# Seven products in place of eight in 16 of the 44 block pairs of the two down projections

## Chip, cores and metric

The kernel runs on one core of one Trainium2 chip. The metric is the device time of one execution in microseconds (us). Of the kernel before there are three runs (median 2378.72 us, 2378.43 to 2379.81) and one profiled execution.

## What is computed

Two transformer blocks on 256 tokens of width 2048, all in float32. The first one mixes (a Mamba-2 head group and a pooling mixer), then comes the gated feed-forward layer that this change touches, then a gated per-layer embedding; the second block is one layer of gated attention and one of retention. Cut to what matters:

```python
def conv_glu(hn, w_up, conv_w, conv_b, w_down):      # hn (256, 2048), w_up (2048, 2*5632), w_down (5632, 2048)
    gate, val = jnp.split(hn @ w_up, 2, axis=-1)
    gate = dwconv_centred(gate, conv_w, conv_b)
    return (jax.nn.gelu(gate, approximate=True) * val) @ w_down
...
h = h + rmsnorm(mix, mix_norm_post)
ff = conv_glu(rmsnorm(h, ffn_norm_pre), w_ffn_up, ffn_conv_w, ffn_conv_b, w_ffn_down)
h = h + rmsnorm(ff, ffn_norm_post)
gate = jax.nn.sigmoid(rmsnorm(h, ple_norm_pre) @ w_ple_gate)
h = h + rmsnorm(gate * (p @ w_ple), ple_norm_post)
```

## The kernel before

**Three products for one.** Every float32 product is made of three TensorE matmuls: each operand is split into a high part (rounded to the fp32r format) and a low part (the rest), and the kernel adds high x high, low x high and high x low in PSUM. Activations (`xa`, `xb`, `xc`) hold both parts side by side; `ff` tile k, 128 of the 5632 inner channels, lies in `xb` or `xc`.

**Pieces.** All weights stream from HBM in one order, `layout()`: the list `uses`, 813 pieces of 128 x 1024 numbers. For piece i SP loads it into `raw[i % 4]` (L624) once the low part of piece i-4 is made; ScalarE makes the high part `whi[i % 6]` (L1049, L1054) once TensorE is done with piece i-6; VectorE makes the low part `wlo[i % 6]` = raw - whi (L1520, L1505: a helper, so most tensor_tensor rows carry that line); TensorE's matmuls of pieces have L702. Each engine runs its own program, a loop over the pieces u: it first makes the split of piece u + 5, then the steps that `at[u]` lists for this point (`late(u, ...)` puts them there). So the order on every engine is fixed by hand, and a step that waits holds up what is behind it on its engine, splits too.

**The feed-forward layer** comes in two halves of 22 `ff` tiles. The up projection of a half has 11 gate and 11 val blocks of four pieces. GpSimd scales them and multiplies gate and value (`gate_scale`, `val_scale`, `val_gate`), VectorE does the convolution taps and the low parts (`val_low`), ScalarE the gelu and the high parts (`val_high`). The last val block of a half is finished by steps placed 1 to 4 pieces into the down projection.

**The down projection** of a half (`down0`, `down1`; `natural_out`, L125) has four blocks c of 512 output columns; a piece holds two k-tiles of one block, and gives 2 k x 2 token halves x 3 = 12 matmuls of 512 columns. Each block has two tiles, token halves t = 0 and 1, in two of the banks 0 to 3 (`bank[n % 4]`, n counts tiles); the first matmul of tile n waits until tile n-4 is evacuated (`emptied`). Banks 4 to 7 are idle there. ScalarE copies `down0` tiles to `sn` (L1275), VectorE adds the `down1` tiles to it (L1939), ScalarE squares the sum, VectorE multiplies it by the norm's row (`weigh`, L1607; the row is loaded into `X` and `ev` by `load_post`, L665).

**Behind it** four `ple` blocks of one piece each run (their tiles need the `down1` banks). VectorE meanwhile finishes the norm and makes the new h (`grow`, L1620, destination hT), TensorE transposes its 128x512 quads (`rms_turn`, L779, L793), the first two after the second ple piece, and the gate projection `pgate` starts on them.

## Time and profile before

| | us |
|---|---|
| median of 3 runs | 2378.72 |
| profiled execution, its own time | 2378.37 |
| its span, first to last instruction | 2376.6 |
| TensorE busy | 2361.9 (11890 matmuls) |
| VectorE busy | 1522.0 |
| ScalarE busy | 1195.6 |
| GpSimd busy | 266.2 |

Times in the rows are us from the start of the span. A row of the timeline gives the start, the length, the engine and line, the operation, output and inputs with their shapes, a count where equal neighbours are merged, and in brackets the idle time before it with who ended it. Neighbouring instructions of an engine overlap by some 0.1 us, so spacing says more than duration. PE is TensorE, DVE VectorE, ACT ScalarE, POOL GpSimd.

### The profile page before, as it was taken

How to read it: one execution, taken by the hardware profiler on the slowest of the kernel's cores; microseconds unless marked ns; L12 is line 12 of the kernel's file. 1: busy time of each engine (PE TensorE's matmuls, PEld its weight loads, DVE VectorE, ACT ScalarE, POOL GpSimd, SP SyncE). 2: the span in 40 equal slices, each digit the busy share in tenths (PEclk: the TensorE clock that was granted, in tenths of full speed). 3: DMA queues.
4: the chain of work that ended last, by engine and by line, in shares of the span. 5: the costliest groups of instructions: out<-in, count | busy, mean ns of one | idle time of the engine just before them, and what ended most of it. 6: DMA issues, size and time to landing. Idle time of an engine off the chain costs nothing.

```text
span 2376.6 us, 29824 instructions
## 1 busy us (share of the span) xinstructions
PE 2361.9 (99%) x11890; PEld 1982.9 (83%) x11890; DVE 1522.0 (64%) x1965; ACT 1195.6 (50%) x1613; POOL 266.2 (11%) x250
## 2 busy tenths in 40 slices
PE   9999999999999999999999999999999999999999
PEld 7878898888888888888788888887888888888887
DVE  7898577675467775575755556657665554656556
ACT  7876454444444444465655555535444444444442
POOL 1262013321013221000000000001000000000000
PEclk9999999999999999999999999999999999999999
DMA  8446656656665666565566565565665666556653
GB/s 297 156 145 198 215 176 195 188 191 192 193 193 187 188 193 207 191 203 175 176 185 205 158 196 162 167 190 164 191 181 180 214 192 197 177 182 182 189 177 125
DMA packets 122940, 444.04 MB, mean 187 GB/s; under 512 B 13744, under 2 KB 15408, under 8 KB 122288
## 3 DMA queue, kind: packets, MB, share of 16 engines
q1 hardware_dynamic: 122800, 442.12, 59.6%
q8 instruction: 94, 1.54, 0.3%
q14 instruction: 46, 0.38, 0.0%
HBM read 439.97 MB, written 2.10 MB: 186 GB/s over the span
## 4 chain that ended last, share of the span: by engine, by line
PE 93%; DVE 4%; ACT 2%; DMA 1%; issue 1%; SPq 0%; DVEq 0%; ACTq 0%
PE bank L702 92%; DVE wlo L1505 1%; DMA raw<-in_w 1%; DVE ev L1508 1%; ACT whi L1054 1%; PE bank L793 0%; DVE hT L1508 0%; DVE hn L1508 0%; PE bank L978 0%; PE bank L1045 0%; DVE xa L1508 0%; ACT hT L1222 0%; PE bank L1000 0%; DMA hT<-in_xT 0%; ACT L1228 0%
## 5 line engine op out<-in xcount | busy, mean ns | idle before, releaser
L1505 DVE TENSOR_TENSOR wlo<-raw,whi 128x1024 fp32r<-128x1024 f32 (+2 forms) x811 | 1012.9, 1252 | 771.2 <-ACT whi L1054 769.2
L1054 ACT ACTIVATE whi<-raw 128x1024 fp32r<-128x1024 f32 (+1 forms) x813 | 854.7, 1054 | 958.9 <-PE bank L702 942.4
L702 PE MATMUL bank<-xa,whi 128*128 128x512 f32 (+1 forms) x2688 | 841.5, 395 | 6.9 <-DVE xa L1508 3.5
L702 PE MATMUL bank<-whi,xa 128*128 128x512 f32 x2048 | 639.4, 393 | 2.2 <-DVE wlo L1505 1.8
L702 PEld LDWEIGHTS bank<-xa,wlo 128*128 128x128 f32 x2656 | 497.5, 188 | 115.0
L702 PE MATMUL bank<-xa,wlo 128*128 128x256 f32 (+1 forms) x2656 | 520.9, 278 | 0.0
L702 PE MATMUL bank<-whi,xb 128*128 128x512 f32 x1536 | 473.8, 390 | 0.0
L702 PEld LDWEIGHTS bank<-whi,xa 128*128 128x128 f32 x2048 | 379.7, 188 | 82.6 <-issue 4.7
L702 PEld LDWEIGHTS bank<-xa,whi 128*128 128x128 f32 x2688 | 411.0, 188 | 16.1 <-issue 6.6
L702 PE MATMUL bank<-wlo,xa 128*128 128x512 f32 x1024 | 399.1, 390 | 0.0
L702 PEld LDWEIGHTS bank<-whi,xb 128*128 128x128 f32 x1536 | 287.3, 188 | 59.3 <-DVE wlo L1505 0.3
L702 PE MATMUL bank<-wlo,xb 128*128 128x512 f32 x768 | 298.9, 389 | 0.0
L702 PEld LDWEIGHTS bank<-wlo,xa 128*128 128x128 f32 x1024 | 192.2, 188 | 41.1
L702 PEld LDWEIGHTS bank<-wlo,xb 128*128 128x128 f32 x768 | 144.1, 188 | 30.3
L2176 POOL TENSOR_TENSOR S<-S,rs 128x256 f32<-128x256 f32 x88 | 103.4, 1198 | 552.7 <-DVE S L1518 439.3
L2176 POOL TENSOR_TENSOR ev<-ev,con 128x256 f32<-128x256 f32 x32 | 40.6, 1288 | 563.4 <-DVE ev L1518 563.4
L2176 POOL TENSOR_TENSOR hn<-hn,hT 128x512 f32<-128x512 f32 x4 | 7.8, 1972 | 725.0 <-DVE xa L1505 724.9
L702 PE MATMUL bank<-whi,xc 128*128 128x512 f32 x224 | 69.1, 390 | 0.0
L1518 DVE TENSOR_REDUCE S<-bank 128x256 f32<-128x512 f32 x88 | 56.4, 681 | 0.9 <-PE bank L702 0.6
L702 PEld LDWEIGHTS bank<-whi,xc 128*128 128x128 f32 x224 | 41.9, 188 | 8.6
L1518 DVE TENSOR_REDUCE ev<-bank 128x256 f32<-128x512 f32 (+1 forms) x66 | 42.5, 683 | 5.7 <-PE bank L702 5.7
L702 PE MATMUL bank<-wlo,xc 128*128 128x512 f32 x112 | 43.6, 389 | 0.0
(244 smaller groups left out, 1264.5 us busy)
## 6 DMA issues: line engine op xcount, KB each, us to landing
raw<-in_w SPq DMA_DIRECT2D x803, 512.0 KB, 3.8
hT<-in_ln_rows SPq DMA_DIRECT2D x2, 2048.0 KB, 8.3
raw<-in_w SPq DMA_DIRECT2D x9, 256.0 KB, 2.8
X<-in_post SPq DMA_DIRECT2D x3, 768.0 KB, 5.5
S<-in_x SPq DMA_DIRECT2D x4, 512.0 KB, 7.8
hT<-in_x SPq DMA_DIRECT2D x1, 2048.0 KB, 8.2
out<-S SPq DMA_DIRECT2D x8, 256.0 KB, 2.5
hT<-in_xT SPq DMA_DIRECT2D x3, 512.0 KB, 6.8
```

Of the source, the lines that this page charges most:

```text
L702: return pe.matmul(o, w, x, start=start, stop=stop, skip_group_check=True)
L1054: act.activation(hi, r, ACT.Copy).then_inc(*w_high(i))
L1505: return dve.tensor_tensor(o, x, y, op)
L1508: return dve.scalar_tensor_tensor(out=o, in0=x, scalar=s, in1=y, op0=op0, op1=op1)
L1518: return dve.tensor_reduce(o, halves(b), AX, ALU.add)
L2176: return pool.tensor_tensor(o, x, y, op)
```

## The change

In both halves `natural_out` gives way to `paired_out`. It takes two neighbouring blocks c together. For four of the eleven k-pairs (`COMBINED`) the 2 x 2 x 2 products (two token halves, two k-tiles, two blocks of columns) are replaced by seven products of sums (the Strassen-Winograd scheme). With the k-tiles' weights as `upper` and `lower`, each with two halves of 512 columns, a group is: `upper` (1 product), `lower` (2), a plain piece, `pair_sums` (2), `full_sums` (2), a plain piece; the remaining k-pairs are plain pieces (2 or 3 ahead of the groups, two in each group, 4 or 3 behind). GpSimd makes the weight sums from the raw pieces (`sums`, four 128x512), ScalarE and VectorE split them as if they were pieces. The `upper` piece is split in its first 512 columns alone. GpSimd also makes the sums of activations (`mixed`, one 128x512 and four 128x128 for each k-pair and half); those of k-pairs 0 and 1 in the up projection, of 2 and 3 in the down projection. Four of the seven products collect in banks 4 to 7; behind the last group `fold` and `fold_end` combine them. In the first half VectorE writes them to `sn` and then adds the tiles there itself (ScalarE does not copy `down0` tiles any more); in the second half they go to a part of `xa`'s space (`wide`) and GpSimd adds them to `sn` (`joined`). The sums of the second half and the norm's row 1 lie in `xa`'s space too. The list has 845 pieces, 813 of them loaded.

```diff
+Use = namedtuple("Use", "mat col k0 n cols block first last part", defaults=("",))
+SUMS = ("pair_sums", "full_sums")
+COMBINED = (0, 1, 2, 3)
+EARLY = (0, 1)
+IN_PAIRS = (0, 1)
...
+    def paired_out(kind, operand, mat, k, start, groups, end):
+
+        begun = len(uses) - 1
+        for c in (0, 2):
+            pair = [begin(kind, c + j, operand, "natural", 512) for j in range(2)]
+            touched, left = set(), [(j, p) for j, p in start + sum([g[1:] for g in groups], ()) + end]
+
+            def plain(j, p):
+                b = pair[j]
+                left.remove((j, p))
+                first, last = j not in touched, j == 1 and (1, p) == end[-1]
+                touched.add(j)
+                use(b, mat, 512 * (c + j), k + 2 * p, 2, first, last)
+
+            def part(name, row, col, first, last=False):
+                uses.append(Use(mat, 512 * (c + col), row, 1, 1024, pair[0], first, last, name))
+                return len(uses) - 1
+
+            for piece in start:
+                plain(*piece)
+            for p, one, two in groups:
+                first, last, row = p == groups[0][0], p == groups[-1][0], k + 2 * p
+                a = part("upper", row, 0, first)
+                late(max(a - 7, begun + 2) if k else a - 7, "sums", a)
+                part("lower", row + 1, 0, first)
+                plain(*one)
+                part("pair_sums", row, 0, first)
+                d = part("full_sums", row, 0, first, last)
+                plain(*two)
+            late(d + 1, "fold", kind, c, d)
+            late(d + 2, "fold_end", kind, c)
+            late(d + 2, kind, pair[0])
+            for piece in end:
+                plain(*piece)
+            assert not left
+        return len(uses) - 1
+
+    def mix(u, half, p):
+        late(u, "mixed", half, p)
+        late(u + 2, "mixed_high", half, p)
...
+            if half in IN_PAIRS and q in EARLY:
+                mix(e + d + 5, half, q)
...
+        if half in IN_PAIRS:
+            n = 2 + half
+            for i, p in enumerate(COMBINED):
+                if p not in EARLY:
+                    mix(len(uses) + n + 6 * (i - 1) - 5, half, p)
+            turns = tuple((j, p) for j in range(2) for p in range(4, 11))
+            ends["down", half] = paired_out(f"down{half}", ("ff",), "w_ffn_down", 22 * half, turns[:n],
+                                            tuple((p, turns[n + 2 * i], turns[n + 2 * i + 1]) for i, p in enumerate(COMBINED)),
+                                            turns[n + 8:])
...
-    late(d - 40, "load_post", 1)
+    late(d - 50, "load_post", 1)
...
+        sums = {0: (X[:, 0:1024], flat(ev[:, 0:4, :])), 1: (wide[:, 0:1024], wide[:, 1024:2048])}
+        mixed_x, mixed_v = flat(sq[:, :, :]), s2[:, 3584:4096]
...
+        def folded(kind, c, t, j):
+            if kind == "down1":
+                return wide[:, 2048 + 1024 * t + 512 * j:2560 + 1024 * t + 512 * j]
+            return sn[:, t, 512 * (c + j):512 * (c + j) + 512]
...
+            w = 512 if s.part == "upper" else s.n * s.cols
+            r = (sum_piece(i) if s.part in SUMS else raw[turn_of[i] % NRAW])[:, 0:w]
+            hi, lo_ = whi[i % NHL][:, 0:w], wlo[i % NHL][:, 0:w]
...
+                    if uses[before].part == "upper":
+                        q.wait_ge(*pool_val.of("sum", before, 2))
+                    elif uses[before].part == "lower":
+                        q.wait_ge(*pool_val.of("sum", before - 1, 4))
+                sp.dma_start(raw[turn % NRAW][:, 0:n], src).then_inc(raw_in[turn % NRAW], 16)
...
+                        if r == 1:
+                            q.wait_ge(*piece_tile.of("used", XA_FREE[1]))
+                            for i in range(2):
+                                sp.dma_start(wide[:, 4096 + 1024 * i:5120 + 1024 * i],
+                                             a["post"][1:2, 1024 * i:1024 * i + 1024].broadcast_to((128, 1024))).then_inc(post_in, 16)
+                            continue
...
+                def product(B, x, c, start, stop=False):
+                    xh, xl = x
+                    mm(B[:, :], xh, hi[:, 512 * c:512 * c + 512], start)
+                    mm(B[:, :], xl, hi[:, 512 * c:512 * c + 512], False)
+                    return mm(B[:, :], xh, lo_[:, 512 * c:512 * c + 512], False, stop)
...
+                if s.part == "upper":
+                    m = product(bank[5], tokens(s.k0, 0), 0, side_free(5), s.last)
+                elif s.part == "lower":
+                    product(bank[n % 4], tokens(s.k0, 0), 0, begins(0))
+                    m = product(bank[(n + 2) % 4], mixture(4), 1, begins(2))
+                elif s.part == "pair_sums":
+                    product(bank[6], mixture(1), 0, side_free(6), s.last)
+                    m = product(bank[4], mixture(3), 1, side_free(4), s.last)
+                else:
+                    product(bank[7], mixture(2), 0, side_free(7), s.last)
+                    m = product(bank[(n + 1) % 4], tokens(s.k0 + 1, 1), 1, begins(1), s.last)
+                m.then_inc(*piece_tile.both(*([("tile", n), ("tile", n + 1)] if s.last else []), ("used", u)))
...
+                if uses[i].part == "pair_sums":
+                    q.wait_ge(*pool_val.of("sum", group_of(i), 2))
+                elif uses[i].part == "full_sums":
+                    q.wait_ge(*pool_val.of("sum", group_of(i), 4))
+                else:
+                    q.wait_ge(*landed(i))
                 if i >= NHL:
                     q.wait_ge(*piece_tile.of("used", i - NHL))
                 act.activation(hi, r, ACT.Copy).then_inc(*w_high(i))
...
+                    elif step == "mixed_high":
+                        half, p = k
+                        q.wait_ge(*pool_val.of("mixed", half, p, 4))
+                        act.activation(mixed_set(half, p)[:, 0, :], mixed_v, ACT.Copy).then_inc(*x_high("mixed", 11 * half + p))
+                    elif step == "fold":
+                        kind, c, d = k
...
+                        q.wait_ge(*piece_tile.of("used", d))
+                        act.activation(folded(kind, c, 0, 0), bank[5][:, :], ACT.Copy).then_inc(*act_evac("first", kind, c))
...
+                    elif step == "mixed_low":
+                        half, p = k
+                        m = mixed_set(half, p)
+                        q.wait_ge(*x_high.of("mixed", 11 * half + p))
+                        tt(m[:, 1, :], mixed_v, f32(m[:, 0, :]), ALU.subtract).then_inc(*x_low("mixed", 11 * half + p))
+                    elif step == "fold":
+                        kind, c, d = k
+                        x = [[folded(kind, c, t, j) for j in range(2)] for t in range(2)]
+                        q.wait_ge(*act_evac.of("first", kind, c))
+                        tt(x[0][1], bank[7][:, :], x[0][0], ALU.subtract).then_inc(*vec_val("less", kind, c))
+                        q.wait_ge(*vec_val.now())
+                        tt(x[1][0], x[0][1], bank[4][:, :], ALU.add).then_inc(*vec_val("fold", kind, c, 0))
+                    elif step == "fold_end":
+                        kind, c = k
+                        x = [[folded(kind, c, t, j) for j in range(2)] for t in range(2)]
+                        q.wait_ge(*vec_val.of("fold", kind, c, 0))
+                        tt(x[0][1], x[0][1], bank[6][:, :], ALU.add).then_inc(*vec_val("fold", kind, c, 1))
+                        tt(x[1][1], x[1][0], bank[6][:, :], ALU.add).then_inc(*vec_val("folded", kind, c))
+                    elif step == "down0" and 0 in IN_PAIRS:
+                        c = k[0].arg
+                        q.wait_ge(*vec_val.of("folded", "down0", c - c % 2))
+                        for t in range(2):
+                            n = k[0].tile + t
+                            x = sn[:, t, 512 * c:512 * c + 512]
+                            q.wait_ge(*piece_tile.of("tile", n))
+                            if t and c % 2 == 0:
+                                tt(x, bank[n % 4][:, :], x, ALU.subtract).then_inc(*vec_evac("tile", n))
+                            else:
+                                tt(x, x, bank[n % 4][:, :], ALU.add).then_inc(*vec_evac("tile", n))
...
+                            if 1 in IN_PAIRS:
+                                q.wait_ge(*pool_val.of("joined", "down1", c - c % 2))
...
+                    elif step == "mixed":
+                        half, p = k
...
+                        tt(r, f32(x[:, :, 0:T]), f32(x[:, :, T:2 * T]), ALU.add).then_inc(*pool_val("mixed", half, p, 0))
+                        upper, lower = mixed_x[:, 0:T], mixed_x[:, T:2 * T]
+                        v = [mixed_v[:, 128 * i:128 * i + 128] for i in range(4)]
+                        q.wait_ge(*pool_val.now())
+                        tt(v[0], upper[:, 128:256], lower[:, 128:256], ALU.subtract).then_inc(*pool_val("mixed", half, p, 1))
+                        tt(v[2], upper[:, 128:256], upper[:, 0:128], ALU.subtract).then_inc(*pool_val("mixed", half, p, 3))
+                        q.wait_ge(*pool_val.of("mixed", half, p, 1))
+                        tt(v[1], upper[:, 0:128], v[0], ALU.subtract).then_inc(*pool_val("mixed", half, p, 2))
+                        q.wait_ge(*pool_val.now())
+                        tt(v[3], lower[:, 0:128], v[1], ALU.subtract).then_inc(*pool_val("mixed", half, p, 4))
+                    elif step == "sums":
...
+                        if earlier:
+                            q.wait_ge(*w_low.of(earlier[-1]))
+                        if uses[a].first and uses[a].col == 0:
+                            q.wait_ge(*(x_low.of("p", 1) if uses[a].block.kind == "down0" else piece_tile.of("used", XA_FREE[1])))
+                        up, low = [raw[turn_of[i] % NRAW] for i in (a, a + 1)]
+                        q.wait_ge(*landed(a))
+                        tt(pair[:, 0:512], up[:, 0:512], up[:, 512:1024], ALU.add).then_inc(*pool_val("sum", a, 1))
+                        q.wait_ge(*landed(a + 1))
+                        tt(pair[:, 512:1024], up[:, 512:1024], low[:, 512:1024], ALU.add).then_inc(*pool_val("sum", a, 2))
+                        q.wait_ge(*pool_val.of("sum", a, 1))
+                        tt(full[:, 0:512], pair[:, 0:512], low[:, 512:1024], ALU.add).then_inc(*pool_val("sum", a, 3))
+                        q.wait_ge(*pool_val.now())
+                        tt(full[:, 512:1024], full[:, 0:512], low[:, 0:512], ALU.add).then_inc(*pool_val("sum", a, 4))
+                    elif step == "fold_end" and k[0] == "down1":
...
+                                q.wait_ge(*vec_val.of("folded", kind, c))
+                                m = tt(x, x, folded(kind, c, t, j), ALU.subtract if (t, j) == (1, 0) else ALU.add)
+                        m.then_inc(*pool_val("joined", kind, c))
```

## Rows read from the trace of the kernel before

**Rows 1.** Page, busy time of TensorE and others, and the granted clock by slice.
```profile
PE 2361.9 (99%) x11890; PEld 1982.9 (83%) x11890; DVE 1522.0 (64%) x1965; ACT 1195.6 (50%) x1613; POOL 266.2 (11%) x250
...
PEclk9999999999999999999999999999999999999999
```
**Rows 2.** Page, the chain that ended last, by engine.
```profile
PE 93%; DVE 4%; ACT 2%; DMA 1%; issue 1%; SPq 0%; DVEq 0%; ACTq 0%
```
**Rows 3.** Timeline of TensorE, two products of the second down projection.
```profile
1031.79 0.61 PE L702 MATMUL bank<-whi,xc 128*128 128x512 f32 x2
1032.24 0.39 PE L702 MATMUL bank<-wlo,xc 128*128 128x512 f32 x1
1032.47 0.61 PE L702 MATMUL bank<-whi,xc 128*128 128x512 f32 x2
1032.92 0.39 PE L702 MATMUL bank<-wlo,xc 128*128 128x512 f32 x1
```
**Rows 4.** Timeline of VectorE, two low parts of the second down projection.
```profile
942.02 1.23 DVE L1505 TENSOR_TENSOR wlo<-raw,whi 128x1024 fp32r<-128x1024 f32 x1 [1.49 <-ACT whi L1054]
944.74 1.23 DVE L1505 TENSOR_TENSOR wlo<-raw,whi 128x1024 fp32r<-128x1024 f32 x1 [1.49 <-ACT whi L1054]
```
**Rows 5.** Timeline of ScalarE, splits behind the second up projection.
```profile
916.45 1.06 ACT L1054 ACTIVATE whi<-raw 128x1024 fp32r<-128x1024 f32 x1 [1.67 <-PE bank L702]
919.17 1.06 ACT L1054 ACTIVATE whi<-raw 128x1024 fp32r<-128x1024 f32 x1 [1.66 <-PE bank L702]
```
**Rows 6.** Windows: length, then PE, PEld, DVE, ACT, POOL busy; second up and down projection.
```profile
661.00:914.00 253.00, 253.00 (x1444) 220.42 (x1443) 174.53 (x220) 112.35 (x136) 64.64 (x62) 1.00 0.61 189
914.00:1033.00 119.00, 119.00 (x527) 98.54 (x526) 63.19 (x61) 51.90 (x59) 4.85 (x4) 1.00 0.64 202
```
**Rows 7.** Timelines of VectorE and GpSimd, and the tile view of hn (min/median/max ns).
```profile
1644.34 10.10 DVE L1505 TENSOR_TENSOR wlo<-raw,whi 128x1024 fp32r<-128x1024 f32 x5 [0.26 <-ACT whi L1054]
1644.22 8.01 POOL L2176 TENSOR_TENSOR hn<-hn,hT 128x512 f32<-128x512 f32 x4 [724.86 <-DVE xa L1505]
L2176 POOL TENSOR_TENSOR hn<-hn,hT x4: 1304/2154/2276, 1644.2 to 1650.1; 128x512 f32<-128x512 f32 x4
```
**Rows 8.** Timelines of VectorE and GpSimd, end of the second up projection (913.7).
```profile
912.61 1.22 DVE L1505 TENSOR_TENSOR wlo<-raw,whi 128x1024 fp32r<-128x1024 f32 x1
913.74 1.28 DVE L1518 TENSOR_REDUCE S<-bank 128x256 f32<-128x512 f32 x2
914.94 1.38 DVE L1505 TENSOR_TENSOR wlo<-raw,whi 128x1024 fp32r<-128x1024 f32 x1
914.51 2.42 POOL L2176 TENSOR_TENSOR S<-S,rs 128x256 f32<-128x256 f32 x2 [8.65 <-DVE S L1518]
916.88 2.48 POOL L2176 TENSOR_TENSOR S<-S 128x256 f32<-128x256 f32 x2
329.74 0.74 POOL L2176 TENSOR_TENSOR S<-S,rs 128x256 f32<-128x256 f32 x1
```
**Rows 9.** Page, DMA issues: count, size, median us to landing.
```profile
raw<-in_w SPq DMA_DIRECT2D x803, 512.0 KB, 3.8
```
**Rows 10.** Groups of VectorE in the second down projection: count, busy, mean ns.
```profile
L1505 DVE TENSOR_TENSOR S<-S,bank 128x512 f32<-128x512 f32 x7 | 4.5, 678 | 0.0
```
**Rows 11.** Timelines of VectorE, ScalarE, TensorE, end of the second down projection.
```profile
1032.92 1.28 DVE L1505 TENSOR_TENSOR S<-S,bank 128x512 f32<-128x512 f32 x2
1034.39 1.31 DVE L1505 TENSOR_TENSOR S<-S,ev 128x512 f32<-128x512 f32 x2 [0.19 <-ACT sq L1101]
1036.39 2.06 DVE L1508 SCALAR_TENSOR_TENSOR hT<-S,sm,hT 128x512 f32<-128x512 f32 x3
1031.76 1.28 ACT L1285 ACT_TABLE_LOAD   x1
1038.59 0.60 PE L793 MATMUL bank<-con,hT 128*128 128x128 f32 x4
```

139 lines of the change are left out of this document (120 added, 19 removed).

## Prediction, made before the changed kernel ran

> **What bounds the kernel now.** I read the page first: TensorE is busy for 2361.9 of 2376.6 us and the clock row shows the upper level (2.4 GHz) in every slice [rows 1]; the chain that ended last is 93% TensorE [rows 2]. So a matmul taken out is worth its spacing, if nothing else gets late. In the timeline of a down projection three matmuls of 512 columns start every 0.68 us, 0.227 us each, 2.72 us for a piece of twelve [rows 3]. VectorE makes one low part per piece and then sits idle 1.49 us for ScalarE, which waits for TensorE to give back a buffer [rows 4, 5]. The splits thus stand at the end of their lead: a piece is split six pieces ahead. The lead, not the mean idle share, is what the change has to live on: it is 16.3 us of TensorE before the change, less the two splits.
>
> Then I looked for GpSimd and VectorE together, because the change gives GpSimd its first work in the down projections (it is idle in the window of the second, after the last two gates) [rows 6]. One place in the trace has wide two-input work on both: GpSimd does four 128x512 operations while VectorE does four low parts and then one more. Alone, a low part occupies 1.13 us (its 1.22 us less the overlap with the next). In this place five of them take 10.10 us, four of them 8.96 us together, 2.24 us each; GpSimd's take a median of 2.15 us and the first 1.30 us [rows 7]. So 1.13 + 1.11 = 2.24: they don't overlap at all, they alternate, one whole instruction each. The end of the second up projection repeats it with 256 columns: the low part at 914.94 takes 1.38 us instead of 1.22 us, and two GpSimd operations 2.42 us, though that form takes 0.74 us where nothing delays it [rows 8]. Reductions that read a bank (913.74) are not stretched.
>
> **What is removed.** Sixteen groups (4 k-pairs, 2 column pairs, 2 halves) need 7 x 3 = 21 matmuls in place of 24: 48 x 0.227 = 10.9 us off TensorE. A group with its two plain pieces has 45 matmuls, 10.2 us. The pieces brought from HBM do not grow in number, and one piece lands in 3.8 us [rows 9].
>
> **What is added to each group.** VectorE: before, four low parts in 10.9 us; now upper (half width, 0.6 us) and lower, one, pair, full, two at 1.13: 6.25 us. GpSimd: four sums of 128x512 at 1.11 us, 4.4 us. Side by side both fit in 10.2 us. As they alternate they need 10.7 us, and there is a loop: the sums of a group wait for the low part of the full sums of the group before (one pair of buffers), and that comes last in VectorE's order. Call the end of that low part F. Without other work F to F is 10.7 to 11.4 us against 10.2; over three steps this costs 1.5 to 3.5 us of a lead of some 9 us. In the second column pair of each half I therefore take nothing (up to 2 us).
>
> **The mixtures left in the down projection** (k-pairs 2 and 3, in the first column pair). Each is a 128x512 and four 128x128 on GpSimd. No row shows a 128x128 there; from 1.11 us for 512 columns and 0.60 us for 256 (the second of the pair in rows 8 ran 0.6 us after the low part ended at 916.32) I get about 0.35 us as an estimate. With the low part of the mixture (0.6 us) the port is asked for 3.1 us more, 13.8 us in such a group. And ScalarE stands in order: the high part of the mixture is queued before the split of pair_sums, so that split, then its low part, start only when the mixture is done: 0.55 + 1.06 us [rows 5] with the port empty. Written out with alternating operations, F to F is 16.3 us (with the two low parts of the last values) and then 15.5 us, against 10.2.
> First half, time from the end of the up projection: the sums of group 1 were made in the up projection, F1 = 5.2 us (used(e+1) at 2.72, high, low), F2 = 21.5, F3 = 37.0. The plain piece of group 4 is then ready after 4 sums and 4.0 us of low parts, at 45.3 us. TensorE would want it at 5.4 + 3 x 10.2 + 2.0 = 38.1. **Loss 7.2 us.** Bounds: if the port never idled 1.8 us, if every sum met a low part 10 us.
> Second half: the sums lie in xa's place and cannot start before the up projection ends, and GpSimd still has the last values, until 4.6 us [rows 8]. Then two sums, split, two sums, split: F1 = 12.7 us, wanted at 14.3. F2 = 29.1, F3 = 44.6, the plain piece 52.9 us, wanted at 8.2 + 30.6 + 2.0 = 40.8. **Loss 12.1 us.** Bounds 6.6 and 16 us. This is the largest term; it shows as waits of TensorE on VectorE of 0.5 to 3 us before lower, one and pair_sums.
> The mixtures of k-pairs 0 and 1 are made in the up projection, where in 253 us VectorE is busy for 175 us [rows 6]; a GpSimd step there is needed four pieces later. Cost nothing; if that cover were gone, 3 us each.
>
> **A rule on this.** The Trainium skill (SBUF — State Buffer, "SBUF: two separate sides") says that a VectorE operation with two SBUF inputs and a GpSimd operation that reads SBUF take one pair of ports exclusively, for the whole instruction. By that rule the sum stands as here; the trace agrees (2.24 us for the pair). If ports were shared freely, the two losses above would be zero.
>
> **Folding, second half.** The output of the first half lies in sn, so GpSimd adds the folded banks to it (four 128x512, "joined"), and VectorE's evacuation of the first block waits for that; low parts are queued behind it on VectorE, squares and splits behind it on ScalarE. From the end of the last combined piece: high and low of the next piece 2.2 us, fold copy, two operations of 0.68 us [rows 10] 3.6, next split 4.9, two more 6.3 us; GpSimd is then still at the sums of the next column pair, which are queued ahead and whose pieces land at 3 and 4.5 us, until 8 to 9.2 us; joined 4 x 1.1 to 1.2: 13 us; evacuation 13.7 us. TensorE has four plain pieces, 10.9 us, then wants that bank. **Loss 3.0 us** (2 to 5). In the first half nothing waits for GpSimd here: evacuated by 8.8 us, wanted at 13.6.
> **At the end** no sums stand in the way: joined by 11.5 us, bank free at 12.3, wanted at 10.9: 1.4 us. But VectorE now comes late to the fourth block: evacuation of the third, weights, two splits, then the fourth at 16.8 us instead of 10.7. From the first evacuation at 1032.92 to the end of the first grown quad (a third of the 2.06 us from 1036.39) are 4.2 us, and the transposes at 1038.59 had only 1.5 us to spare [rows 11]. They move from 16.3 to about 21.3 us. **Loss 5.0 us** with the 1.4 (3 to 8). What is late next is the table load of 1.28 us on ScalarE before the squares [rows 11], hidden behind the splits.
>
> Moves with one answer: the norm row goes to xa's place, the same bytes on SP's queue, ten pieces into the second down projection (some 22 us), wanted first by the weights behind the first folding (46 us): nothing. Evacuations of the first half go from ScalarE to VectorE, 8 x 0.68 us where it idles 1.49 us per piece: nothing.
>
> **Sum.** Against the profiled execution, 2378.4 us (span 2376.6, 1.8 around it; the median of the runs is 2378.7): 2378.4 - 10.9 + 7.2 + 12.1 + 3.0 + 5.0 = **2394.8 us**. Lower bounds 1.8 + 6.6 + 2 + 3 give 2380.9; upper ones 10 + 16 + 5 + 8 give 2406.
>
> **Rivals.** Differences within 0.2%, 4.8 us, count as no change.
> A, faster: the sums and low parts overlap after all, for instance because GpSimd reads other buffers than VectorE. It speaks for it that rows 7 and 8 are few; against it, that they also have different buffers on the two engines (hn and raw, S and raw). Then F to F is 4.4 + 1.06 + 1.13 = 6.6 us, the groups lose nothing, and only the foldings stay, some 1.5 + 3: 2372 us. If even these are hidden 2367.5 us. It decides once F to F is under the lead's allowance, about 12 us for a group with a mixture. Chance 0.10.
> B, the lead covers the groups (the port is fair but GpSimd's operations fall into VectorE's idle time), and the foldings cost their 8 us: 2375.5 us, or a few us more with a part of the second half's loss. For it: VectorE idles 55% of a plain piece. Against it: in a group VectorE's and GpSimd's work is 10.7 of 10.2 us. Chance 0.14.
> C, forecast: the shared port stretches the first column pair of both halves: 2381 to 2405 us, 2395 likeliest. Chance 0.70.
> D, worse: the sums come late in the second column pairs too, since loads wait for sums (raw slots of upper and lower are held until the second and fourth sum, then 3.8 us), so that each of eight more groups loses 1 to 2 us: 2405 to 2412 us. Chance 0.06.
> That fewer matmuls are removed than said: the page must count 11842 in place of 11890; the blocks of the diff give that number, so I leave it no chance of its own.
> The range reaches over B and C: 2375 to 2405. Faster 0.10 (A, most of it), within 0.2% 0.16 (B and the low edge of A and C), slower 0.74.
>
> **What will show it.** Low parts in the groups at 2.2 us beside sums of 2.2 us, and at 1.2 us elsewhere: the port. TensorE's waits on VectorE's low parts in the first 50 us of both down projections, more in the second (7 and 12 us), next to none in the second column pairs: the loop. One wait on an evacuation, 3 us, at the change of column pair in the second half, and one before the ple blocks; first transposes 5 us later relative to the last down matmul: the folding. No TensorE idle time in the first column pairs would make the forecast wrong; sums of 1.2 us beside low parts of 1.2 us would tell why.

## The result, and the profile after

| | before | after |
|---|---|---|
| median of 4 runs | 2379.26 us | 2407.09 us (2406.81 to 2408.38) |
| profiled execution | 2378.4 us, span 2376.6 | 2408.4 us, span 2406.6 |
| matmuls | 11890 | 11842 |

The changed kernel is slower: the ratio is 1.0117, 95% interval 1.0105 to 1.0130. The forecast was 2394.8 us with a range of 2375 to 2405, and the measured time lies above it, at a time that the prediction had given to its rival D. The sign held, the size did not: 16 us of loss were foreseen and 28 came. The page of the kernel after, its busy times and its clock:

```profile
PE 2364.6 (98%) x11842; PEld 1977.8 (82%) x11842; DVE 1626.4 (68%) x2029; ACT 1218.4 (51%) x1649; POOL 429.8 (18%) x362
...
PEclk9999999999999999999999999999999999999999
```

Against [rows 1] there are 48 matmuls fewer, so the change does what it says, and TensorE is nevertheless "busy" 2.7 us longer. The difference between span and busy time of TensorE went from 14.7 to 42.0 us. VectorE has 104 us more work and GpSimd 164 us.

**Where the time lies.** The two stages that the change touches, as windows (length, then busy time of PE, PEld, DVE, ACT, POOL, the granted clock of TensorE, DMA share, GB/s): the first down projection, and the second one with the ple blocks up to the first transposes.

```profile
550.05:673.40 123.35, 117.75 (x506) 95.33 (x505) 106.39 (x82) 61.24 (x68) 65.45 (x42) 0.99 0.55 181
918.60:1067.50 148.90, 128.07 (x531) 101.61 (x529) 111.56 (x96) 68.41 (x87) 79.35 (x54) 0.95 0.52 170
```

Before, the same two stages took 119.7 us (528 matmuls) and 125.1 us (the transposes at 1038.59 [rows 11]). 504 matmuls are worth 114.3 us, so the first one now holds 9.1 us in which TensorE waited or ran slowly; of the second, 119.7 us are matmuls and 29.2 us are loss. The second up projection between them takes 245.2 us in both traces. In each stage the loss is its length less its matmuls at 0.2267 us. The sum for the profiled execution: 2378.4 - 10.9 (matmuls) + 9.1 + 29.2 + 1.5 (a stretch at 181 us, below) + 1.0 (behind the transposes) = 2408.3 us, against 2408.4.

**The waits.** TensorE's timeline of after, only its rows that carry a wait (start, length, instruction, then the idle time ahead and what ended it). The first column pair of the first half, then that of the second half, the change of column pair of the second half, and its end:

```profile
571.46 0.73 PE L824 MATMUL bank<-whi,xs 128*128 128x512 f32 x2 [0.82 <-DVE wlo L1712]
580.50 0.74 PE L824 MATMUL bank<-whi,xc 128*128 128x512 f32 x2 [0.57 <-DVE wlo L1712]
587.66 1.22 PE L824 MATMUL bank<-whi,xs 128*128 128x512 f32 x2 [4.11 <-DVE wlo L1712]
...
938.81 0.73 PE L824 MATMUL bank<-whi,xb 128*128 128x512 f32 x2 [1.48 <-DVE wlo L1712]
941.04 0.73 PE L824 MATMUL bank<-whi,xb 128*128 128x512 f32 x2 [1.26 <-DVE wlo L1712]
946.59 0.73 PE L824 MATMUL bank<-whi,xs_ev 128*128 128x512 f32 x2 [1.15 <-DVE wlo L1712]
955.63 0.72 PE L824 MATMUL bank<-whi,xb 128*128 128x512 f32 x2 [0.57 <-DVE wlo L1712]
962.80 1.07 PE L824 MATMUL bank<-whi,xa 128*128 128x512 f32 x2 [4.14 <-DVE wlo L1712]
...
996.88 1.19 PE L824 MATMUL bank<-whi,xb 128*128 128x512 f32 x2 [8.37 <-DVE S L1712]
...
1058.83 1.19 PE L824 MATMUL bank<-whi,xc 128*128 128x512 f32 x2 [2.55 <-DVE S L1712]
1064.13 0.70 PE L824 MATMUL bank<-whi,xc 128*128 128x512 f32 x2 [0.85 <-DVE S L1712]
1067.57 0.65 PE L973 MATMUL bank<-con,hT 128*128 128x128 f32 x4 [0.45 <-DVE hT L1715]
```

"DVE wlo" is a low part that was late: the loop of sums and splits. "DVE S" is an evacuation into sn, so a bank that was not yet free: the folding. The bracket leaves out the end of the matmul before; measured from start to start less one spacing, the four large waits cost 4.3, 4.3, 8.5 and 2.7 us. The second column pairs have no wait inside them. Cut at these rows, with 252 matmuls (57.1 us) to a column pair and 24 to the two ple pieces, the 29.2 us of the second stage are 12.5 us in the first column pair, 10.6 us at the change (8.5 of wait and 2.1 behind it) and 6.0 us at the end, to 0.1 us.

**The port.** Timelines of VectorE and GpSimd of after inside a group of the second half:

```profile
948.19 7.39 DVE L1712 TENSOR_TENSOR wlo<-raw,whi 128x1024 fp32r<-128x1024 f32 x4
948.35 3.92 POOL L2418 TENSOR_TENSOR wide<-raw 128x512 f32<-128x512 f32 x2 [4.69 <-DVE wlo L1712]
952.24 4.49 POOL L2418 TENSOR_TENSOR wide<-wide,raw 128x512 f32<-128x512 f32 x2
```

The single low parts inside the first row, at 951.05 and 953.28, take 2.31 and 2.30 us, the sums at 952.24 and 954.58 take 2.27 and 2.15; elsewhere a low part takes 1.22 us as in [rows 4]. It is the picture of [rows 7].

**The change of column pair.** GpSimd of after from 973 to 996 us; then SP's queue and VectorE at the rows that decide when those sums can start; and one group of the view of waits between 950 and 1000 us (who waited for what: us in total, times, longest):

```profile
984.99 1.29 POOL L2418 TENSOR_TENSOR wide<-raw 128x512 f32<-128x512 f32 x1 [12.06 <-DMA raw<-in_w]
986.79 1.74 POOL L2418 TENSOR_TENSOR wide<-raw 128x512 f32<-128x512 f32 x1 [0.50 <-DMA raw<-in_w]
988.48 2.60 POOL L2418 TENSOR_TENSOR wide<-wide,raw 128x512 f32<-128x512 f32 x2
991.04 4.92 POOL L2418 TENSOR_TENSOR S<-S,wide 128x512 f32<-128x512 f32 x4
...
973.00 0.33 SPq L747 DMA_DIRECT2D raw<-in_w  x1
977.78 2.49 DVE L1712 TENSOR_TENSOR wlo<-raw,whi 128x1024 fp32r<-128x1024 f32 x2 [0.23 <-ACT whi L1239]
980.30 0.33 SPq L747 DMA_DIRECT2D raw<-in_w  x1
982.41 0.33 SPq L747 DMA_DIRECT2D raw<-in_w  x1
...
SPq L448 <- POOL wide L2418: 14.0, 5, 4.1
```

The last combined piece was used at about 977.5 us. The folded banks were complete 11 us behind that, at 988.6. GpSimd began the next column pair's sums 7.5 us behind it, because their first piece landed only then (the second at 9.3 us); its four additions to sn ended at 995.96, and VectorE evacuated at 996.05. Why the pieces were late can be followed through the slots. The last sum of the group before ended at 972.93, and only then was the slot of lower free: SP issued the next load at 973.00 and the one queued behind it right after. These two pieces landed, were split, and their low parts ended at 980.27 (the row at 977.78). The slot of the second was the one that the next column pair's upper needed, so its load went out at 980.30 and landed at 984.99; that of lower went out at 982.41, behind one more low part. So two loads stand one behind the other between the last sum of one column pair and the first of the next, and GpSimd has nothing to do for 12.06 us. The row of SP's queue has the held loads: five times one waited for a sum, up to 4.1 us.

**The clock.** Not foreseen: behind each of the four large waits TensorE runs at half its clock. Windows of after: before the wait, right behind it, and a little later; then behind the wait that ended at 587.66.

```profile
980.00:988.00 8.00, 8.00 (x37) 6.64 (x36) 6.22 (x8) 3.56 (x4) 2.51 (x2) 1.00 0.88 301
996.90:1000.50 3.60, 3.60 (x9) 2.83 (x10) 3.23 (x5) 2.67 (x6) 0.00 (x0) 0.50 0.10 8
1002.00:1010.00 8.00, 8.00 (x37) 6.58 (x36) 6.58 (x8) 6.01 (x10) 2.64 (x2) 1.00 0.49 149
587.70:591.00 3.30, 3.30 (x8) 2.62 (x9) 3.30 (x4) 2.96 (x4) 1.57 (x1) 0.51 0.00 0
```

A granted clock of 0.50 is the lower level, 1.2 GHz; a matmul of 512 columns then starts every 0.43 us instead of 0.227. Such a stretch costs 1.6 to 1.8 us here, together 6.7 of the 38.3 us. The view counts these matmuls as busy, which is why PE's busy time grew while its work shrank. The page's row of the clock, in slices of 60 us, doesn't show it. The 1.5 us ahead of the first down projection are the same thing: at 181.5 us, in code that the change doesn't touch, this execution ran at 0.50 for some 3 us behind a wait with 1.55 us of idle time, and the profiled execution of before did not. Other kernels below have it in some executions too; it is no effect of the change.

### The profile page after: what moved, and what is told of

It reads as the page before. It is cut to its first block, busy times and chain, and to the rows that moved or that the text cites. A ratio compares the mean times of both kernels' runs of the same rounds, so it can differ in the third digit from the quotient of the medians.

```text
span 2406.6 us, 30013 instructions
## 1 busy us (share of the span) xinstructions
PE 2364.6 (98%) x11842; PEld 1977.8 (82%) x11842; DVE 1626.4 (68%) x2029; ACT 1218.4 (51%) x1649; POOL 429.8 (18%) x362
## 4 chain that ended last, share of the span: by engine, by line
PE 54%; DVE 1%; ACT 0%; issue 0%; DVEq 0%; ACTq 0%
PE bank L824 53%; DVE wlo L1712 0%; DVE hn L1715 0%; PE bank L1225 0%; PE bank L1158 0%; PE bank L973 0%; PE bank L1180 0%; ACT whi L1239 0%; DVE xa L1712 0%; DVE S L1712 0%; ACT S L1268 0%; DVE sm L1760 0%; ACT wide L1287 0%; PE bank L1005 0%; ACT L1536 0%
## 5 line engine op out<-in xcount | busy, mean ns | idle before, releaser
L1712 DVE TENSOR_TENSOR wlo<-raw,whi 128x1024 fp32r<-128x1024 f32 (+2 forms) x811 | 1047.1, 1299 | 656.0 <-ACT whi L1239 654.0
L1239 ACT ACTIVATE whi<-raw 128x1024 fp32r<-128x1024 f32 (+2 forms) x813 | 844.1, 1045 | 864.0 <-PE bank L824 823.0
L824 PE MATMUL bank<-whi,xa 128*128 128x512 f32 x2080 | 650.6, 394 | 6.5 <-DVE wlo L1712 5.9
L824 PEld LDWEIGHTS bank<-whi,xa 128*128 128x128 f32 x2080 | 386.2, 188 | 89.4 <-DVE wlo L1712 7.0
L824 PE MATMUL bank<-whi,xb 128*128 128x512 f32 x1376 | 426.8, 391 | 11.7 <-DVE S L1712 8.4
L824 PE MATMUL bank<-wlo,xa 128*128 128x512 f32 x1040 | 406.0, 390 | 0.0
L824 PEld LDWEIGHTS bank<-whi,xb 128*128 128x128 f32 x1376 | 257.7, 188 | 68.0 <-issue 8.8
L824 PE MATMUL bank<-wlo,xb 128*128 128x512 f32 x688 | 268.6, 390 | 0.0
L824 PEld LDWEIGHTS bank<-wlo,xb 128*128 128x128 f32 x688 | 129.5, 188 | 27.2
```

The costliest lines, as they stand in the source:

```text
L824: return pe.matmul(o, w, x, start=start, stop=stop, skip_group_check=True)
L1239: act.activation(hi, r, ACT.Copy).then_inc(*w_high(i))
L1712: return dve.tensor_tensor(o, x, y, op)
```

## Experiments

The kernel before ran beside each of them, with a median between 2378.6 and 2379.3 us. Ratios are against it, with 95% intervals. "Cost" of a wait is start to start less one spacing, plus the slow stretch behind it.

Theory: in the first column pair of each half VectorE's and GpSimd's operations alternate on one port, and the late mixtures (k-pairs 2 and 3) push the loop over what TensorE's work covers; the foldings add their waits in the second half. Rival 1: the port is not the cause; buffers, loads or the order on ScalarE are. Rival 2: the change could not gain at all, since each microsecond saved comes back at a later wait.

### Each half by itself

```diff
-IN_PAIRS = (0, 1)
+IN_PAIRS = (0,)
```

> The changed kernel with the seven products in the first half alone; the second down projection is that of the kernel before. Theory (shared port of VectorE and GpSimd, and ScalarE's order, in the first column pair): the first half cost 9 us of waits for 5.4 us saved in the changed kernel's trace, so the kernel is 3 to 4 us slower than before: 2382 to 2384 us. Rival (the changed code outside the down projections costs too, such as the mixtures made in the up projection): 2385 us or more. Rival (the first half is a gain by itself): under 2377 us.

Measured 2388.6 us, 1.0041 (1.0026 to 1.0055): a miss. The first down projection was the same as in the changed kernel, and one more wait stood in the plain second one:

```profile
927.98 0.74 PE L824 MATMUL bank<-whi,xb 128*128 128x512 f32 x2 [3.78 <-DVE wlo L1712]
```

It is an artefact of the edit. The change lets the row's load stand 50 pieces before the end of the down projection; with the 44 whole pieces that the second one now has again, that place is six pieces inside the up projection. There SP waits for xa to be free, with all the later loads queued behind. The repeat puts only that back:

```diff
-    late(d - 50, "load_post", 1)
+    late(d - 40, "load_post", 1)
```

> Seven products in the first half alone, as before, but the norm row is loaded 40 pieces ahead of the end, not 50. In the kernel with 50 its wait for the end of the second up projection stood on SP's queue six pieces ahead of that end, as the second down projection is 44 pieces there. Theory: that is a mistake of that experiment, its wait of 4.2 us with the slow stretch behind it at the start of the second down projection goes, and what stays is the first half's own cost: 2382 to 2384 us. Rival (the change costs outside the down projections): 2386 us or more.

Measured 2382.1 us, 1.0014 (1.0005 to 1.0024). TensorE has three waits for low parts in the first down projection and none in the second. View of waits, first down projection of this kernel:

```profile
PE bank L824 <- DVE wlo L1712: 5.3, 3, 4.2
```

So the first half alone costs about 3 us (2.8 by the medians, 3.5 in the profiled execution, where the stage loses 8.9 us and 24 matmuls give back 5.4). The other 25 us belong to the second half. The pair also shows the price of a step moved past a queue: 6.5 us for the place of one load.

### The port alone

In the kernel before, GpSimd gets 32 operations of 128x512 in each down projection, four at a time, on a part of s2 that nobody else uses. Nothing waits for them within the stage.

```diff
+                    elif step == "extra":
+                        half, i = k
+                        q.wait_ge(*w_low.of(u))
+                        for n in range(4):
+                            q.wait_ge(*pool_val.now())
+                            tt(s2[:, 3584:4096], s2[:, 3584:4096], s2[:, 3584:4096], ALU.add).then_inc(*pool_val("extra", half, i, n))
```

> The kernel before, with 8 times four additions of 128x512 on GpSimd in each down projection, on a buffer that nothing else uses, once every five pieces (13.6 us). No engine waits for them. Theory: low parts beside them take 2.2 us in place of 1.2 us, and TensorE does not notice, since the lead of six pieces covers it and nothing is queued behind: 2378 to 2380 us. So the shared port alone, without the waits that the change builds on it, costs nothing. Rival (the port by itself delays TensorE): 2383 us or more.

Measured 2378.6 us, 0.9997 (0.9987 to 1.0006). VectorE and GpSimd of this kernel:

```profile
927.01 6.02 DVE L1508 TENSOR_TENSOR wlo<-raw,whi 128x1024 fp32r<-128x1024 f32 x3
936.57 1.82 DVE L1508 TENSOR_TENSOR wlo<-raw,whi 128x1024 fp32r<-128x1024 f32 x1 [1.50 <-ACT whi L1056]
925.76 6.18 POOL L2179 TENSOR_TENSOR S<-S 128x512 f32<-128x512 f32 x4
935.16 6.26 POOL L2179 TENSOR_TENSOR S<-S 128x512 f32<-128x512 f32 x4 [3.21 <-DVE wlo L1508]
```

GpSimd touches only its own buffer and VectorE's low parts are stretched all the same, three of them to 6.0 us instead of 3.5, and the operations of GpSimd to 1.5 us on average instead of 1.1. So they alternate on separate buffers too; rival A of the prediction had held it possible that they would not. By itself the stretching costs TensorE nothing: 1.22 us of low part per 2.72 us leave room. That it becomes a wait with a group's extra VectorE work and its loop is an inference: no run has the groups without the alternation. The Trainium skill's rule that was weighed in the prediction (SBUF — State Buffer, "SBUF: two separate sides": one engine has the pair for the whole instruction, the other is fully blocked) is borne out by these rows.

### The late mixtures

The mixtures of k-pairs 2 and 3 are left out, and their products read those of k-pairs 0 and 1; nothing else changes.

```diff
                 if p not in EARLY:
-                    mix(len(uses) + n + 6 * (i - 1) - 5, half, p)
+                    pass
...
-                    q.wait_ge(*x_low.of("mixed", s.k0 // 2))
-                    m = mixed_set(int(b.kind == "down1"), x)
+                    q.wait_ge(*x_low.of("mixed", 11 * int(b.kind == "down1") + x % 2))
+                    m = mixed_set(int(b.kind == "down1"), x % 2)
```

> The changed kernel without the mixtures of k-pairs 2 and 3 (20 GpSimd operations, 4 high and 4 low parts left out); their products read the mixtures of k-pairs 0 and 1 instead, so part of the down projections is computed from other numbers, with the same matmuls, weight sums and splits. Theory (mixtures on the shared port, and the split of pair_sums queued behind them on ScalarE, stretch the loop from 11 to 16 us): the waits of the first column pairs go almost whole (9 and 12 us), and as VectorE is no longer behind, the change of column pair in the second half costs 3 to 5 us in place of 10.7; the end costs its 6 us: 2379 to 2386 us. Rival (weight sums and raw slots held for them are the cause): it stays over 2395 us.

Measured 2389.4 us, 1.0043 (1.0028 to 1.0058), 17.7 us less than the changed kernel and outside the 2379 to 2386 expected. In the first down projection TensorE has no wait left: 114.3 us for its 504 matmuls. In the second the first column pair costs 2.7 us instead of 12.5. So four late mixtures cost TensorE 18.9 us in the first column pairs, and the sums without them 2.7 us. The edit takes out the mixtures' work on GpSimd, ScalarE and VectorE at once; it doesn't say which of the three weighs most. What I expected to shrink with them and did not is the wait at the change of column pair:

```profile
977.49 1.19 PE L824 MATMUL bank<-whi,xb 128*128 128x512 f32 x2 [8.69 <-DVE S L1712]
965.97 3.17 POOL L2418 TENSOR_TENSOR wide<-raw 128x512 f32<-128x512 f32 x2 [13.31 <-DMA raw<-in_w]
```

With its lead intact the wait is as long as before. GpSimd again starts the next sums 8.2 us after the last combined piece (at about 957.8), when their piece lands. So this wait does not come from lateness carried over; it is made on the spot.

Queueing only the high and low part of a late mixture three pieces later, so that ScalarE's split of pair_sums stands ahead of it:

```diff
+        d = 0 if p in EARLY else 3
-        late(u + 2, "mixed_high", half, p)
-        late(u + 3, "mixed_low", half, p)
+        late(u + 2 + d, "mixed_high", half, p)
+        late(u + 3 + d, "mixed_low", half, p)
```

> The changed kernel, but the high and low parts of the two late mixtures of each half are queued three pieces later on ScalarE and VectorE, behind the splits of pair_sums and full_sums. Theory (ScalarE's order holds up the split of pair_sums until the mixture is done): the loop of such a group shrinks by 2 to 3 us, four times: 8 to 12 us less in all, 2395 to 2399 us. Rival (only the port counts, and the same work stands on it): 0 to 4 us less, 2403 us or more.

Measured 2401.2 us, 1.0093 (1.0076 to 1.0110). The first down projection lost 7.2 us in place of 9.1, the first column pair of the second half 12.0 in place of 12.5, and the change of column pair 7.4 in place of 10.6; in all less than expected. The order on ScalarE is worth about a fifth of the first half's loss; in the second half, where the sums start later, hardly anything in the groups.

### The folding at the change of column pair

Three edits at this wait. First, the four additions to sn are made by VectorE right behind the folding, not by GpSimd behind the next sums:

```diff
                         tt(x[1][1], x[1][0], bank[6][:, :], ALU.add).then_inc(*vec_val("folded", kind, c))
+                        if kind == "down1":
+                            q.wait_ge(*vec_val.now())
+                            for t in range(2):
+                                for j in range(2):
+                                    y = sn[:, t, 512 * (c + j):512 * (c + j) + 512]
...
+                            m.then_inc(*vec_val("joined", kind, c))
```

> The changed kernel, but the four additions of the folded banks to sn in the second half are made by VectorE right behind the folding, not by GpSimd behind its weight sums. Theory (GpSimd's queue decides: 2.5 us of sums and 5 us of additions stand between folding and evacuation): the bank at the change of column pair is free 5 us earlier, at the end 2.7 us earlier, with the slow stretch of TensorE behind each wait shorter too: 9 to 11 us less, 2396 to 2398 us. Rival (VectorE's lateness decides, and 2.5 us more work on it makes that worse): 3 us less at most, 2404 us or more.

Measured 2402.8 us, 1.0101 (1.0086 to 1.0116): 4.3 us less than the changed kernel, not the 9 to 11 expected. At the change 6.00 us of idle time stayed, 9.1 us with the slow stretch, which was longer here (2.9 us). Second, GpSimd keeps the additions but makes them ahead of the next column pair's sums:

```diff
-                late(max(a - 7, begun + 2) if k else a - 7, "sums", a)
+                late((max(a - 7, begun + 2) if c == 0 else max(a - 7, d0 + 3)) if k else a - 7, "sums", a)
```

> The changed kernel, but in the second half GpSimd's additions of the folded banks at the change of column pair stand ahead of its weight sums for the next pair. In the changed kernel the sums waited for their pieces until 7.5 us after the last combined piece, ended at 13.6 us, and the additions at 18.5 us, while the folding was done at 11 us. Theory (two parts: pieces and so the folding late by loads held for sums, and GpSimd's queue): the queue's part is the 2.5 us between 11 and 13.6 us; the bank is free 2.5 us earlier and the rest of the wait, 6 us, stays: 2403 to 2406 us. Rival (the queue is all of it): the wait of 8.5 us and the slow stretch go, 2397 us or less.

Measured 2407.0 us, 1.0120 (1.0106 to 1.0134): nothing gained. TensorE of this kernel, the change of column pair and the end:

```profile
992.52 1.19 PE L825 MATMUL bank<-whi,xb 128*128 128x512 f32 x2 [5.49 <-DVE S L1713]
1057.34 1.19 PE L825 MATMUL bank<-whi,xc 128*128 128x512 f32 x2 [5.44 <-DVE S L1713]
```

Of 8.37 us of idle time at the change 5.49 stayed, about as expected, and the end went from 2.55 to 5.44 us: the 2.9 us won at the one place are lost at the other. (All times of this trace are 1.5 us earlier, for lack of the stretch at 181 us; with that taken off, the bank at the end came free at the same time as in the changed kernel, to 0.1 us.) What stays at the change are the additions themselves, behind a folding that is late, not GpSimd's queue; GpSimd of this kernel:

```profile
986.67 4.92 POOL L2419 TENSOR_TENSOR S<-S,wide 128x512 f32<-128x512 f32 x4 [15.28 <-DVE wide L1713]
```

They start with the end of the folding and end at 991.59, and TensorE's bank is free a microsecond later. Third, VectorE frees the bank first, adding it to the folded buffer, and adds to sn afterwards:

```diff
-                            q.wait_ge(*pool_val.of("joined", "down1", c - c % 2))
-                            tt(x, x, bank[n % 4][:, :], ALU.add).then_inc(*vec_evac("tile", n))
+                            x = folded("down1", c - c % 2, t, c % 2)
+                            tt(x, x, bank[n % 4][:, :], ALU.subtract if t and c % 2 == 0 else ALU.add).then_inc(*vec_evac("tile", n))
+                        for t in range(2):
...
+                            tt(x, x, folded("down1", c - c % 2, t, c % 2),
+                               ALU.subtract if t and c % 2 == 0 else ALU.add).then_inc(*vec_val("joined", c, t))
```

> The changed kernel, but in the second half VectorE adds the banks of a block to the folded buffer first (which frees them) and then adds the folded buffer to sn itself; GpSimd's additions are gone and no evacuation waits for another engine. Theory (the bank was held from the folding through GpSimd's weight sums and additions): the bank at the change of column pair is free at the folding, about when TensorE wants it, and at the end no bank is late: of the 10.3 and 6.5 us that these two places cost in the changed kernel's trace 1 to 2 us each stay: 2391 to 2394 us. Rival (VectorE, late because pieces land late, is what holds TensorE there whoever adds): 5 us less at most, 2402 us or more.

Measured 2400.9 us, 1.0090 (1.0075 to 1.0105): 6.2 us less than the changed kernel where 13 to 16 were expected. (The whole edit also moves the scratch of the squares out of xa's space and lets each square wait for the one before it.) TensorE in the first column pair of the second half, with the granted clock behind that wait; then at the change, soon behind it, and at the end:

```profile
940.49 1.22 PE L824 MATMUL bank<-whi,xb 128*128 128x512 f32 x2 [1.26 <-DVE wlo L1715]
...
940.50:943.20 2.70, 2.70 (x6) 2.14 (x7) 1.33 (x1) 0.06 (x1) 2.52 (x4) 0.50 0.76 259
...
988.99 0.70 PE L824 MATMUL bank<-whi,xb 128*128 128x512 f32 x2 [0.27 <-DVE wide L1715]
1001.94 1.22 PE L824 MATMUL bank<-whi,xb 128*128 128x512 f32 x2 [2.48 <-DVE wlo L1715]
1056.74 1.19 PE L824 MATMUL bank<-whi,xc 128*128 128x512 f32 x2 [3.23 <-DVE wide L1715]
```

Of the 10.6 us at the change half a microsecond stays, and 4.2 us come back at 1002 us (2.6 of wait and 1.6 at the lower clock): the low parts there are now late. Two causes are possible and not told apart: VectorE has four more additions queued ahead of them, and the wait at the change no longer gives the engines behind TensorE their lead back. About 2 us more are lost where the edit changes nothing, since the slow stretches behind the low parts' waits of the two first column pairs are longer or more in this execution (the row at 940.49 has one, the changed kernel at the same wait none).

### Fewer groups, where there is room

If the loop is the cause, fewer groups and a longer lead of whole pieces in the first column pair remove it. On top of the edit above: two groups (k-pairs 0 and 1, whose mixtures come from the up projection) behind six whole pieces in the first column pair, four groups in the second; the late mixtures are then made while whole pieces run. 36 matmuls fewer.

```diff
-                    mix(len(uses) + n + 6 * (i - 1) - 5, half, p)
+                    mix(len(uses) + 9 + 3 * (i - 2), half, p)
...
+            for ps, n in ((EARLY, 6), (COMBINED, n)):
+                turns = tuple((j, p) for j in range(2) for p in range(11) if p not in ps)
+                plans.append((turns[:n], tuple((p, turns[n + 2 * i], turns[n + 2 * i + 1]) for i, p in enumerate(ps)),
+                              turns[n + 2 * len(ps):]))
```

> As the kernel that frees the banks first, and with two groups (k-pairs 0 and 1) in the first column pair of each half, four in the second; mixtures 2 and 3 are made beside plain pieces. 12 groups, 36 matmuls fewer than before: 8.2 us. Theory (the waits came from mixtures between sums on the shared port, and from banks held): nearly no waits are left, 0 to 3 us: 2370 to 2374 us, faster than the kernel before. Rival (groups stretch TensorE by themselves, by loads held for sums): 2378 us or more.

Measured 2380.6 us, 1.0006 (0.9997 to 1.0015): 26.5 us less than the changed kernel, but above the 2370 to 2374 us expected, and not to be told from the kernel before. The first down projection is clean; the second has waits of 1.4 us inside and loses 6.5 us at its end, where the bank is late; that end was not in the expectation:

```profile
1035.90 1.19 PE L826 MATMUL bank<-whi,xc 128*128 128x512 f32 x2 [3.75 <-DVE wide L1717]
```

Fewer whole pieces at the start of the second column pair, so two or three more behind its groups to cover the last folding:

```diff
-            for ps, n in ((EARLY, 6), (COMBINED, n)):
+            for ps, n in ((EARLY, 6), (COMBINED, 2 - half)):
```

> The kernel with two and four groups and banks freed first, but its second column pairs begin with two plain pieces in the first half and one in the second, so that one or two pieces more stand behind the last group, 16.3 us of TensorE behind the folding in the second half in place of 10.9 us. Its trace had 6 us of waits left at the end of the second half, where VectorE came to the last bank 4 us late because folding, additions, squares and weights of the block before stood ahead. Theory (that queue): they go but for about 1 us, 2373 to 2376 us, faster than before by 3 to 6 us. Rival (the work of the end on VectorE is simply too much for the ple pieces to cover): 2379 us or more.

Measured 2381.4 us, 1.0011 (1.0002 to 1.0020). Again a miss. The end shrank from 6.5 to 3.2 us (1.2 before the bank, 2.0 before the transposes), and the groups, which have now a shorter lead, wait 4.2 us between 962 and 1008 in place of 1.4. In the second half 18 matmuls (4.1 us) bring 7.3 us of waits.

So the last two runs drop the second half altogether and keep two and four groups in the first one, where no sum waits for xa's place and no addition to sn is needed:

```diff
-IN_PAIRS = (0, 1)
+IN_PAIRS = (0,)
...
-    late(d - 50, "load_post", 1)
+    late(d - 40, "load_post", 1)
```

> The groups in the down projection of the first half only: two groups in its first column pair, behind six whole pieces, four in its second; the second down projection as before the change and the load of the row at d-40. 18 matmuls fewer (4.1 us). In the kernel with this order in both halves the first down projection ran without any wait, and everything that was lost stood in the second. So: 2378.8 - 4.1 = 2374.7, range 2373.5 to 2376.5. Rival (what is saved here comes back at a later wait whatever is done, as every kernel so far has ended at or above the time of the kernel before): 2377.5 to 2380.

Measured 2375.27 us, 0.9984 (0.9975 to 0.9993): 3.4 us faster than the kernel before, the only version that beats it, though by less than the 0.2% that the prediction calls a change. Its first down projection as a window, and below it the same stage in the kernel before:

```profile
550.30:666.30 116.00, 116.00 (x513) 95.79 (x512) 96.90 (x79) 58.80 (x64) 57.14 (x37) 1.00 0.60 195
...
548.50:668.20 119.70, 119.70 (x530) 99.14 (x529) 56.27 (x49) 50.95 (x53) 4.87 (x4) 1.00 0.63 192
```

TensorE is busy for all of it at full clock. VectorE is busy for 97 of 116 us, in the kernel before for 56 of 120. Rival 2 falls with this run: what is saved stays saved where nothing waits. The same with one more group in the first column pair, whose mixture must be made while groups run:

```diff
-            for ps, n in ((EARLY, 6), (COMBINED, n)):
+            for ps, n in (((0, 1, 2), 6), (COMBINED, n)):
```

> As the one with two and four groups in the first down projection alone, but three groups in its first column pair, behind the same six whole pieces: 21 matmuls fewer (4.8 us), and one mixture (k-pair 2) is formed and split while that column pair runs. By theory the port is then shared for one group of sums and one mixture longer, and the lead of six pieces (over 6 us) covers it: 2374.0, range 2373 to 2376. Rival: the mixture formed beside the sums brings waits back as it did in the change (9.1 us for four groups with two late mixtures): 2376 to 2379.

Measured 2381.55 us, 1.0009 (1.0000 to 1.0018): above even the rival's range, and the run that says most about the loop. Three matmuls fewer (0.7 us) cost 6.3 us. TensorE and GpSimd of this kernel:

```profile
589.33 0.73 PE L826 MATMUL bank<-whi,xb 128*128 128x512 f32 x2 [1.26 <-DVE wlo L1714]
593.89 0.73 PE L826 MATMUL bank<-whi,xb 128*128 128x512 f32 x2 [2.88 <-DVE wlo L1714]
...
573.04 2.28 POOL L2420 TENSOR_TENSOR sq<-xb 128x512 f32<-128x512 f32 x1
575.40 2.72 POOL L2420 TENSOR_TENSOR S<-sq 128x128 f32<-128x128 f32 x2
578.08 1.98 POOL L2420 TENSOR_TENSOR S<-sq,S 128x128 f32<-128x128 f32 x2
580.01 2.56 POOL L2420 TENSOR_TENSOR X<-raw 128x512 f32<-128x512 f32 x2
582.51 2.28 POOL L2420 TENSOR_TENSOR ev<-X,raw 128x512 f32<-128x512 f32 x1
584.87 1.63 POOL L2420 TENSOR_TENSOR ev<-ev,raw 128x512 f32<-128x512 f32 x1
```

The third group's sums can begin only at 580.01, behind a mixture that took GpSimd 7 us (573.04 to 580.06), and in the kernel with two groups the same mixture ran with nothing behind it. It cost 4.5 us of waits and a slow stretch of 1.7 us. A lead of six pieces wasn't enough for one mixture in a loop that just fits without it.

## Why the prediction came out as it did

**What held.** The matmuls taken out, 48, are worth 10.9 us. VectorE and GpSimd alternate by whole instructions (2.27 beside 2.31 us, forecast 2.2 and 2.2). The waits stand where the forecast put them: low parts in the first column pairs, none in the second ones, an evacuation at the change of column pair of the second half, one before the ple blocks.

**The first column pairs** were forecast at 7.2 and 12.1 us of loss and measured 9.1 and 12.5. The loop itself was well written out. The low parts of the full sums ended 5.4, 23.1 and 39.3 us after the up projection in the first half, against 5.2, 21.5 and 37.0, and 13.1, 29.6 and 45.8 us in the second, against 12.7, 29.1 and 44.6. The price of a sum was a little low: 1.11 us, where four additions in a row with VectorE idle took 4.92 us, 1.23 each. 1.7 us of either loss are TensorE at the lower clock, which was in no term. The share of the late mixtures, argued in the prediction, is shown by the run without them: 9.1 to 0 and 12.5 to 2.7. How much of it is the shared port, and how much the order on ScalarE and the chain of sums and splits, is in part open: the later high parts brought 2.4 us of it back, and no run has the mixtures without the alternation.

**The step that failed is the folding at the change of column pair**: 3.0 us forecast, "2 to 5" as its bounds, 10.6 measured (8.5 of wait, 2.1 behind it, nearly all of that at the lower clock). The forecast let the pieces of the next column pair land at 3 and 4.5 us after the last combined piece, so that GpSimd was done with the sums by 8 to 9.2 us and with the additions by 13; they landed at 7.5 and 9.3, the sums ended at 13.6 and the additions at 18.5. The price of one landing was about right (the median is 3.9 us on the page of after, 3.8 in [rows 9]; these two took 4.7 and 4.4). What was left out is that the loads could not be issued: the slot of lower was held for the last sum of the group before, and the slot that the next upper needed was emptied only after the pieces held up by that had landed and been split. That is the mechanism of the prediction's rival D, loads that wait for sums, which I had placed in the second column pairs with a chance of 0.06 and not at their border. The measured time lies in D's range of 2405 to 2412, but D's place was wrong: no wait stands inside a second column pair. The same late pieces held the splits, so the folding too was complete at 11 in place of 6.3 us. That the wait is not lateness carried over from the mixtures is shown by the run without them, where its idle time is 8.7 us against 8.4. The run with the additions ahead of the sums splits it: 2.9 us of it are GpSimd's queue, and 5.5 us are the additions behind a late folding. That held slots make the pieces late is read from the rows; a run with more raw slots, which would show how much of the wait goes with them, was not made.

**The end** was forecast at 5.0 us and measured 6.0 (2.7, 1.6 at the lower clock, 1.0 and 0.6), inside its bounds of 3 to 8; without the lower clock it would be 4.4.

**The sum of the misses**: 1.9 + 0.4 + 7.6 + 1.0, with 2.5 us outside the two stages (1.5 at 181 us, which varies between executions, and 1.0 behind the transposes), makes 13.4 us of the 13.6 by which the profiled execution lies over the forecast. The upper bound of 2405 failed by 2 us. The prediction's own upper terms gave 2406, and 2367.5 + 10 + 16 + 5 + 8 is 2406.5; the range was drawn a little inside that. The bound of the folding at the change, 5 us, was the one that reality went past, and no slow stretch stood in any of them: the four of the two stages cost 6.7 us.

**The signs.** A (the two engines' operations overlap) is refuted by the rows at 948 us and by the run with the port alone. B (the lead covers the groups) is refuted for the change as it is, but the run with two and four groups in the first half shows what B described: 97 us of VectorE in 116 us and not one wait.

## What to carry to other kernels

That an engine's mean share is low doesn't make added work on it free: write the loop out between the two engines that share a port, with its buffers, its loads and its in-order queues, and compare one turn of it with TensorE's work in that turn. A step moved or a slot held longer is priced by everything that stands behind it in the queue of loads (6.5 us for the place of one row's load; the change of column pair cost 7.6 us more than forecast, with its slots held for sums). If a turn just fits, adding one more user tips it: one group for 0.7 us of matmuls cost 6.3 us, while six groups with their mixtures made beside whole pieces gained 3.4 us.

## What the runs showed of the hardware

- TensorE's granted clock falls to 0.50 behind waits in the middle of a busy stream, at a price that no sum should leave out. Behind the waits with 8.4, 4.1, 4.1 and 2.55 us of idle time in the changed kernel the matmuls started every 0.43 us for 1.6 to 1.8 us of loss each; over all the kernels such a stretch has 6 to 14 matmuls and costs 1.3 to 3.0 us. The length of the wait alone doesn't decide it. Waits of 0.5 to 1.5 us were mostly followed by none, but the one of 1.26 us in the kernel that frees the banks first was; one of 2.16 us in the kernel with later high parts was, and one of 2.22 us in the kernel where VectorE makes the additions was not. Behind a wait of 1.5 us that ends near 181 us, the same in all kernels, some executions show it (1.4 us and more) and others don't.
- The alternation between VectorE and GpSimd on separate buffers goes by whole instructions: 1.22 and 1.1 us become 2.3 us each, also where one of the two has half the columns (a GpSimd operation of 128x128 takes 0.46 us alone and 1.3 to 1.4 us beside 1.48 us low parts, at 575 to 578 us in the last run).
- Stretching a neighbour's low parts does not by itself move the end: 64 added GpSimd operations of 128x512 changed the time by -0.03% (interval -0.13% to +0.06%).
